# Expert weights of a mixture-of-experts layer: one 1 MB transfer a unit in place of two of 512 KB

## What is computed

```python
def _moe(h, router_w, router_b, exp_gate, exp_up, exp_down):
    ...
    for e in range(N_EXPERTS):
        y = y + combine[..., e:e + 1] * _swiglu(h, exp_gate[e], exp_up[e], exp_down[e])
    return y
```

## Time and profile before

| | |
|---|---|
| median of three runs (lowest to highest) | 1851.77 us (1849.15 to 1852.33) |
| the profiled execution's own time | 1850.45 us |
| its span, first to last instruction | 1848.6 us |
| busy share of the span: TensorE, VectorE, ScalarE | 91%, 68%, 54% |
| read from memory | 426.59 MB |
| mean granted TensorE clock | 0.954 |

### The profile page before, as it was taken

How to read it: one execution, slowest core, us unless ns; L and a number is a source line. 1 busy time by engine, 2 the same in 40 slices (tenths; PEclk the granted TensorE clock), 3 DMA queues, 4 the chain that set the end, 5 groups by cost and what they waited for, 6 DMA issues and landing times.

```text
span 1848.6 us, 20707 instructions
## 1 busy us (share of the span) xinstructions
PE 1686.5 (91%) x7867; PEld 1393.6 (75%) x7867; DVE 1249.3 (68%) x1518; ACT 991.9 (54%) x1322; POOL 89.1 (5%) x99
## 2 busy tenths in 40 slices
PE   5889988899999978999799998999999999999890
PEld 4777767778778768998677777888787888888780
DVE  5575346655363356775655456899898999998886
ACT  5753253253343243443543445777777777777770
POOL 1002300110000000000000000000000000000003
PEclk9989998899999998999799999999999999999995
DMA  9543144378354325555245557999999999999983
GB/s 327 175 146 129 53 146 143 103 246 300 114 176 146 112 102 182 182 184 205 95 129 184 186 172 249 369 381 380 369 368 361 366 376 380 370 383 373 345 326 114
DMA packets 205227, 436.58 MB, mean 236 GB/s; under 512 B 13375, under 2 KB 46762, under 8 KB 205098
## 3 DMA queue, kind: packets, MB, share of 16 engines
q1 hardware_dynamic: 195050, 398.20, 61.6%
q0 software_dynamic: 8352, 30.42, 4.8%
q10 hardware_dynamic: 1696, 6.29, 0.9%
HBM read 426.59 MB, written 20.86 MB: 242 GB/s over the span
## 4 chain that ended last, share of the span: by engine, by line
PE 79%; DVE 8%; ACT 4%; issue 3%; DMA 3%; POOL 1%; SPq 0%; DVEq 0%; ACTq 0%; POOLq 0%
PE ps L511 24%; PE ps L513 23%; PE ps L512 23%; DVE w_lo L434 4%; PE ps L695 2%; ACT w_hi L428 2%; PE ps L1157 2%; PE ps L696 2%; DMA raw<-in_exp_up 1%; ACT hf L1418 1%; PE ps L924 1%; DMA raw<-in_exp_gate 1%; PE ps L723 1%; PE ps L1312 0%; DMA raw<-in_w_mod 0%
## 5 line engine op out<-in xcount | busy, mean ns | idle before, releaser
L434 DVE TENSOR_TENSOR w_lo<-raw,w_hi 128x1024 fp32r<-128x1024 f32 (+1 forms) x760 | 894.2, 1216 | 245.4 <-ACT w_hi L428 238.3
L428 ACT CAST w_hi<-raw 128x1024 fp32r<-128x1024 f32 (+1 forms) x760 | 767.8, 1047 | 401.8 <-PE ps L513 269.2
L511 PE MATMUL ps<-w_hi,gT_hi 128*128 128x512 f32 x792 | 316.6, 400 | 18.1 <-issue 8.9
L513 PE MATMUL ps<-w_hi,gT_lo 128*128 128x512 f32 x792 | 310.7, 392 | 0.0
L512 PE MATMUL ps<-w_lo,gT_hi 128*128 128x512 f32 x792 | 310.3, 392 | 0.0
L511 PE MATMUL ps<-w_hi,prodT_hi 128*128 128x512 f32 x528 | 211.5, 401 | 8.8 <-DVE prod_dense L2146 5.2
L513 PE MATMUL ps<-w_hi,prodT_lo 128*128 128x512 f32 x528 | 207.6, 393 | 0.0
L512 PE MATMUL ps<-w_lo,prodT_hi 128*128 128x512 f32 x528 | 206.9, 392 | 0.0
L511 PEld LDWEIGHTS ps<-w_hi,gT_hi 128*128 128x128 f32 x792 | 150.0, 189 | 50.9 <-issue 10.1
L513 PEld LDWEIGHTS ps<-w_hi,gT_lo 128*128 128x128 f32 x792 | 149.7, 189 | 32.2
L512 PEld LDWEIGHTS ps<-w_lo,gT_hi 128*128 128x128 f32 x792 | 150.2, 190 | 29.6
(11 more groups left out here) (356 smaller groups left out, 1860.3 us busy)
## 6 DMA issues: line engine op xcount, KB each, us to landing
raw<-in_exp_gate SPq DMA_DIRECT2D x176, 512.0 KB, 5.7
raw<-in_exp_up SPq DMA_DIRECT2D x176, 512.0 KB, 5.7
raw<-in_exp_down SPq DMA_DIRECT2D x176, 512.0 KB, 5.3
raw<-in_w_mod SPq DMA_DIRECT2D x96, 512.0 KB, 4.8
y_rows<-in_exp_up POOLq DMA_DIRECT2D x8, 1536.0 KB, 28.1
raw<-in_w_in_conv SPq DMA_DIRECT2D x24, 512.0 KB, 6.5
raw<-in_ffn_gate SPq DMA_DIRECT2D x22, 512.0 KB, 4.8
raw<-in_ffn_up SPq DMA_DIRECT2D x22, 512.0 KB, 5.6
```

Source lines behind the costliest of these rows:

```text
L428: nc.scalar.copy(w_hi[:, s, cols], raw[:, n % RAW, cols]).then_inc(sem("w_hi_ready"), 1)
L434: nc.vector.tensor_tensor(w_lo[:, s, cols], raw[:, n % RAW, cols], w_hi[:, s, cols].bitcast(F32), ALU.subtract).then_inc(sem("w_ready"), 1)
L511: nc.tensor.matmul(out, a[0], b[0], start=start, stop=False)
L513: return nc.tensor.matmul(out, a[1], b[0], start=False, stop=stop)
```

## The change

The 31 units of an expert that hold one matrix are loaded by one transfer of 1 MB. It waits for both halves of unit n - 3, and ScalarE waits once, for the whole unit. Units 26 and 27 (`NARROW`) keep two transfers, both issued after one wait for the whole of unit n - 3; the second half has a landing semaphore of its own. The other layers' units are loaded as before.

```diff
--- before.py
+++ after.py
@@ -70,6 +70,7 @@
 CHUNKS = len(CHUNK_PAIRS)
 FFN_UNITS = 3 * PAIRS
 GATHER_AT = FFN_UNITS - 5
+NARROW = (26, 27)
 
 
 MOD_CHUNKS = [(layer, v, h) for layer in (0, 1) for v in range(6) for h in (0, 1)]
@@ -201,16 +202,16 @@
 CONST, CONST_AT, MASKS, RET_TABLES, RANKS = _constants()
 
 
-def weight_unit(w, n, expert=None):
+def weight_unit(w, n, expert=None, whole=False):
 
     def halves(mat, c0, width, k0, nk):
         half = (nk + 1) // 2
         src = mat.rearrange("(k p) n -> p k n", p=P)
-        return [(b - a, src[:, k0 + a:k0 + b, c0:c0 + width]) for a, b in ((0, half), (half, nk))]
+        return [(b - a, src[:, k0 + a:k0 + b, c0:c0 + width]) for a, b in (((0, nk),) if whole else ((0, half), (half, nk)))]
 
     def rows(mat, k0):
         src = mat.rearrange("(k p) n -> p k n", p=P)
-        return [(1, src[:, k0 + a:k0 + a + 1, :]) for a in (0, 1)]
+        return [(2, src[:, k0:k0 + 2, :])] if whole else [(1, src[:, k0 + a:k0 + a + 1, :]) for a in (0, 1)]
 
     def ffn(gate, up, down, i):
         for phase in (0, 1):
@@ -424,7 +425,12 @@
             if n >= SPLIT:
                 act.wait_ge(sem("w_used"), val(n - SPLIT + 1, FFN_UNITS, e))
             for part, cols in enumerate(unit_parts(n)):
-                act.wait_ge(sem(f"raw_landed{n % RAW}_{part}"), val(16 * (n // RAW + 1), 16 * FFN_UNITS // RAW, e))
+                if n >= U_MOE and part:
+                    more, u = divmod(n - U_MOE, FFN_UNITS)
+                    if u in NARROW:
+                        act.wait_ge(sem(f"narrow_landed{u}"), 16 * ((e or 0) + more + 1))
+                else:
+                    act.wait_ge(sem(f"raw_landed{n % RAW}_{part}"), val(16 * (n // RAW + 1), 16 * FFN_UNITS // RAW, e))
                 nc.scalar.copy(w_hi[:, s, cols], raw[:, n % RAW, cols]).then_inc(sem("w_hi_ready"), 1)
 
         def dve_split(dve, n, e=None):
@@ -531,6 +537,16 @@
 
         @block.sync
         def _(sp):
+            def load_whole(u, e):
+
+                n = U_MOE + u
+                sp.wait_ge(sem("w_ready"), val(2 * (n - RAW) + 2, 2 * FFN_UNITS, e))
+                parts = weight_unit(t, n, e, whole=u not in NARROW)
+                each = UNIT // len(parts)
+                for part, (nk, src) in enumerate(parts):
+                    dst = raw[:, n % RAW, part * each:(part + 1) * each].rearrange("p (k n) -> p k n", k=nk)
+                    sp.dma_start(dst, src).then_inc(sem(f"narrow_landed{u}" if part else f"raw_landed{n % RAW}_0"), 16)
+
             def load(n, e=None):
                 for (nk, src), (part, cols) in zip(weight_unit(t, n, e), enumerate(unit_parts(n))):
                     if n >= RAW:
@@ -557,7 +573,7 @@
                 load(n)
             for e in range(N_EXP):
                 for u in range(FFN_UNITS):
-                    load(U_MOE + u, e)
+                    load_whole(u, e)
             for i in range(TILES):
                 sp.wait_ge(sem(f"y_ready{i}"), 1)
                 dst = outs[0][0] if i == 0 else outs[1][0, (i - 1) * P:i * P, :]
```

## The result

The changed kernel took **1899.43 us** (median of four runs, 1897.24 to 1904.52) against 1852.05 for the kernel before: 1.0258 of it, interval 1.0239 to 1.0277. That is 47 us slower where 14 were forecast, and 3 us above the upper end of the range.

A forecast was written before the change was run, and what follows sets the result against it. TensorE was taken to bound the kernel, with experts 1 to 7 deciding. Per expert 2.8 + 0.8 - 1.5 = 2.1 us, 15 us for seven, added to 1850.45 and adjusted to the median, gave 1866 us; range 1856 to 1896.

The forecast's parts named there:

- The bound before: Experts 1 to 7 before the change: TensorE sets the pace at 2.90 us a unit, transfers do not.
- expert 0: Two tiles give TensorE twice the work a unit, transfers have half their rate spare: the change costs nothing there.
- The ring of three buffers: Raw weight buffers, from a load's issue until its buffer is free again: predicted 8.56 us, with 8.70 allowed.
- L: Transfer time of one 1 MB weight load: taken as 5.08 us, between 3.9 and 5.9; up to 5.2 allowed.
- Store and gather: Each expert's 512 KB store to y_rows and gather of next token rows: 1.38 us each, no longer hidden.
- the product: VectorE's 0.63 us product no longer fits between two units' subtracts: 6 x 0.14 = 0.8 us an expert.
- The sum for one expert: Experts 1 to 7: delays of 2.8 and 0.8 us less 1.5 us in hand, a loss of 2.1 us each.
- the prediction's sign of being right: In the profile after: 35 issues an expert, 1 MB landing in about 5.1 us, more TensorE waits for VectorE's split.
- no change: Whole kernel at 1852 us, if 1 MB lands in 4.6 us or less or TensorE's lead absorbs delays; chance 0.20.
- faster: Expert boundaries: a shallower queue shortens the "issue" stops, saving 8 us, 1844 us in all; chance 0.12.
- Much slower: Experts 1 to 7: 1 MB loads take 5.4 us or more, stalls may lower TensorE's clock; 1896 us and more; chance 0.13.
- the heavy case: The outcome of 1896 us and more, with 1 MB loads of 5.4 us or above; chance 0.13.

The follow-up runs named there:

- lean kernels: Changed kernel and kernel before, each without the gather of token rows and storing only 128 of 1024 columns of each expert's sums: 1877.45 and 1849.31 us.

## Why the prediction was right or wrong

- **The bound before, and expert 0**: right. TensorE set the pace; a fourth buffer gains nothing, and expert 0 takes as long as before in the windows.
- **What decides**: right. The ring of three buffers is what the change lengthens; a fourth gives all 47 us back.
- **L, a single load of 1 MB**: right. In expert 0, where loads stand alone, the changed kernel's DMA issues at 1018.1 and 1066.5 are

```profile
raw<-in_exp_up SPq DMA_DIRECT2D x1, 1024.0 KB, 5.1
...
raw<-in_exp_down SPq DMA_DIRECT2D x1, 1024.0 KB, 5.0
```

against 5.08 predicted; from expert 0's unit 8 on all of them took 4.8 to 5.4. The formula of the Trainium skill (DMA: Bandwidth & Descriptors, "Anatomy of one DMA") is a fit for transfers that GpSimd issues. For these, which SyncE issues, its 4.4 us was 0.6 to 0.7 too short, and its 3.2 for 512 KB 0.4 to 0.5.

- **Store and gather, 2.8 us an expert**: right, 7 x 2.8 = 20 us against 19 net by the lean kernels; with an interval of 9 us to either side the closeness is luck. That the later waits take ScalarE's and VectorE's other work along is seen in TensorE's waits for the product.
- **The sum for one expert: the ring at 2.853 a unit with 1.5 us in hand**: this step failed. It put the load at 5.08 for every unit, as if nothing ever met a load. In the changed kernel the mean load is 5.81 (medians 5.2 to 5.8, where the prediction's sign of being right was about 5.1). Without store and gather the mean load is still 5.51 and from landing to the end of the split it takes 3.66, not 3.45: 0.03 + 5.51 + 3.66 = 9.2 us a round, 3.07 a unit, and the trace has 3.05. Instead of 1.5 us in hand that is 33 x 0.15 = 5 us lost an expert, less what the product was given (0.8): 29 us for seven, against the 25 that stay without store and gather.
- Why a load takes longer there than alone is read from the lean changed kernel's trace, not tested. Of its 182 loads of 1 MB from expert 2's unit 4 on (5.48 us in the mean), 89 met no packet of another queue, and the load ahead of them landed less than 3 us after their issue: 5.15. Another 19 met none either, but the load ahead landed later: 5.95. This is bunching: loads are issued when VectorE finishes a unit, and two splits in a row can end 2.4 us apart, while a load needs 2.8 of the transfer engines (512 KB at 379 GB/s is 1.38), so the second waits. The other 74 met an instruction fetch of 16 or 8 KB: 5.76. Of the 0.40 us above 5.08 the bunched loads carry about a quarter by these counts, the loads that met a fetch two thirds. How far a fetch delays a load by itself stays open.
- **The rivals**: no change and faster didn't come. "Much slower" has the right size, 1891 to 1896 us, by a wrong road: L alone is not 5.4, and the clock played a small part. In experts 1 to 7 of the profiled executions it was at 0.50 for 17.0 us, before for 10.2, which at half the speed is 3 of the 47 us. The stop at expert 7's start is still there, with ScalarE idle 4.66 us for "issue" (before 5.89), so a shallower queue did not remove it.
- Two small slips change nothing: 1850.45 + 15 + 1.3 is 1866.8, and the loader waited before all of its 344 issues (345 is the count of half splits).
- **The range** ended at 1896 because the heavy case was held to be rare. A ring within 2% of the pace that it has to keep was a sign that irregular arrivals would decide, and they can only lose.

## What to carry to other kernels

Before two transfers are made one, work out the round of their buffer: landing, every step that now waits for the whole, and the release; compare it with the number of buffers times the pace of the bound engine. If it comes out within some per cent of that, count the loads at their mean in a stream, not at the time of a single one, and expect a loss. The larger transfer is better by itself (some 16 us here, with equal waits); it wants one more buffer to pay for the coarser hand-over, and even then it gains nothing where another engine is the bound.

## What was not expected of the hardware

Seven extra copies of 512 KB cost the kernel before 10 us, and thirty-five of 16 KB 7 us, though TensorE hardly waited for its weights there; why is open. And in the changed kernel copies of 16 KB in one packet left the mean load at 5.85 us, the same bytes in sixteen packets at 5.88, where it was 5.81 without them.
